# Strassen's weight sums ahead of the value, x's sums in a part's second couple: the order of two engines' queues in a float32 block on one Trainium2 core

## The reference

```
for l in range(2):
    x = x + 0.5 * swiglu(rms_norm(x, norm_ffn1[l]), ffn1_w_gate[l], ffn1_w_up[l], ffn1_w_down[l])
    x = x + hybrid_mixer(...)
    x = x + 0.5 * swiglu(rms_norm(x, norm_ffn2[l]), ffn2_w_gate[l], ffn2_w_up[l], ffn2_w_down[l])

swiglu(x) = (silu(x @ w_gate) * (x @ w_up)) @ w_down      # 1024 -> 2816 -> 1024, float32
```

## Time and profile before

| | us |
|---|---|
| three runs | 2627.64, 2631.72, 2637.26 (median 2631.72) |
| the profiled execution | 2631.17 |
| its span in the profile | 2629.4 |
| busy in it: PE, DVE, ACT, POOL | 2509.1 (95%), 1686.7 (64%), 1042.7 (40%), 248.3 (9%) |

### The profile page before, as it was taken

The page is one execution under the profiler, slowest core; times in us unless marked ns, Lnnn a source line. Parts: engine busy times, 40 slices in busy tenths (PEclk is TensorE's granted clock), DMA queues, the critical chain, the costliest instruction groups (busy, mean ns, idle before and its releaser), DMA issues. The chain is left out here.

```text
span 2629.4 us, 36570 instructions
## 1 busy us (share of the span) xinstructions
PE 2509.1 (95%) x14533; PEld 2120.8 (81%) x14533; DVE 1686.7 (64%) x2268; ACT 1042.7 (40%) x1434; POOL 248.3 (9%) x178
## 2 busy tenths in 40 slices
PE   7997997999999999999999999999999999999998
PEld 6876776888887878778888878888887777788886
DVE  5355996667675443658676787777743446777776
ACT  4344884333243234544343343333412255433333
POOL 0002112600003300120000010000050001100000
PEclk9998998999999999999999999999999999999999
DMA  4215994322324321232323233232333213232322
GB/s 140 65 56 208 399 412 159 96 89 97 97 91 134 101 73 52 77 97 72 98 98 105 85 97 97 96 98 96 120 108 88 66 35 98 85 101 92 110 83 80
DMA packets 88897, 292.72 MB, mean 111 GB/s; under 512 B 11523, under 2 KB 16531, under 8 KB 88467
## 3 DMA queue, kind: packets, MB, share of 16 engines
q1 hardware_dynamic: 81634, 264.10, 31.3%
q0 software_dynamic: 6224, 23.60, 2.3%
q10 hardware_dynamic: 864, 2.62, 0.2%
HBM read 276.12 MB, written 12.58 MB: 110 GB/s over the span
## 5 line engine op out<-in xcount | busy, mean ns | idle before, releaser
L507 DVE TENSOR_TENSOR w_lo<-w_raw,w_hi 128x1024 fp32r<-128x1024 f32 (+2 forms) x372 | 456.5, 1228 | 155.5 <-ACT w_hi L502 154.2
L551 PE MATMUL bank_l<-xg_hi,w_hi 128*128 128x512 f32 (+1 forms) x1312 | 515.5, 393 | 17.4 <-DVE w_lo L507 15.3
L502 ACT ACTIVATE w_hi<-w_raw 128x1024 fp32r<-128x1024 f32 (+2 forms) x372 | 370.7, 1005 | 364.5 <-PE bank_l L551 342.7
L551 PE MATMUL bank_l<-xg_lo,w_hi 128*128 128x512 f32 (+1 forms) x1312 | 510.0, 389 | 0.0
L551 PE MATMUL bank_l<-xg_hi,w_lo 128*128 128x512 f32 (+1 forms) x1312 | 507.1, 387 | 0.0
L551 PEld LDWEIGHTS bank_l<-xg_hi,w_hi 128*128 128x128 f32 x1312 | 247.5, 189 | 77.5 <-DVE w_lo L507 15.3
L551 PEld LDWEIGHTS bank_l<-xg_lo,w_hi 128*128 128x128 f32 x1312 | 247.3, 189 | 52.9 <-issue 2.2
L551 PEld LDWEIGHTS bank_l<-xg_hi,w_lo 128*128 128x128 f32 x1312 | 247.7, 189 | 52.1
L551 PE MATMUL bank_l<-hid_hi_ff,w_hi 128*128 128x512 f32 x704 | 279.2, 397 | 0.6 <-DVE hid_lo_ff L637 0.6
L551 PE MATMUL bank_l<-hid_hi_ff,w_lo 128*128 128x512 f32 x704 | 278.7, 396 | 0.0
L551 PE MATMUL bank_l<-hid_lo_ff,w_hi 128*128 128x512 f32 x704 | 276.6, 393 | 0.0
(11 more groups left out here) (436 smaller groups left out, 4810.0 us busy)
## 6 DMA issues: line engine op xcount, KB each, us to landing
w_raw<-in_ff_gate SPq DMA_DIRECT2D x88, 512.0 KB
expert_raw<-in_experts SPq DMA_DIRECT2D x81, 512.0 KB, 19.8
w_raw<-in_in SPq DMA_DIRECT2D x80, 512.0 KB
w_raw<-in_ff_down SPq DMA_DIRECT2D x64, 512.0 KB
up_raw<-in_ff_up SPq DMA_DIRECT2D x52, 512.0 KB, 4.6
w_raw<-in_ff_up SPq DMA_DIRECT2D x36, 512.0 KB
w_raw<-in_out SPq DMA_DIRECT2D x24, 512.0 KB
w_raw<-in_ff_down SPq DMA_DIRECT2D x32, 384.0 KB
```

The source lines that it names most:

```text
L502: act.activation(split_memory(i)[0], split_part(i), ACT.Copy).then_inc(*panel_hi.done(i))
L507: dve.tensor_tensor(lo, split_part(i), hi.bitcast(F32), ALU.subtract).then_inc(*panel_lo.done(i))
L551: done = pe.matmul(dst, w[:, c * cols:(c + 1) * cols], moving, start=c == 0 and n == 0, stop=c == kc - 1 and n == 2)
```

## The change

For the plain couple ahead of a couple by seven (j = 2, 5, 10, 13, 18), the order on DVE was S1, S3, value, S2, S4, rest of the value, rest of pair 0. It becomes S1, S3, S2, S4, rest of pair 0, value, rest of the value. On ACT the rounding of pair 0 comes before that of the value.

x's sums: T1 and T3 were made in the part's second couple (j = 1, in ff1_0 j = 6) behind the gate's scaling and the panel split, T2 and T4 in the third (j = 2, in ff1_0 7). Now T1 and T3 are made ahead of the second couple's gate scaling, T2 and T4 behind its panel split, and only their rests but for T1's stand in the third couple. On ACT, T1 and T3 are rounded ahead of `round_ahead(up)`, T2 and T4 behind it, all in the second couple.

```
--- before.py
+++ after.py
@@ -2008,21 +2008,21 @@
                         continue
                     gate, up = ff_keys(stage, j)
                     round_ahead(act, gate)
-                    if j == SEVEN[stage][0] - 1:
-                        round_x_sum(act, stage, "T2")
-                        round_x_sum(act, stage, "T4")
                     if j == 0 and before == "n":
                         first_root_act(act)
                     elif j == 0:
                         root_of_sum(act, before)
                     silu_act(act, stage, j)
-                    round_ahead(act, up)
                     if j == SEVEN[stage][0] - 2:
                         round_x_sum(act, stage, "T1")
                         round_x_sum(act, stage, "T3")
-                    hidden_act(act, stage, g, i, j)
+                    round_ahead(act, up)
+                    if j == SEVEN[stage][0] - 2:
+                        round_x_sum(act, stage, "T2")
+                        round_x_sum(act, stage, "T4")
                     if by_seven_next(stage, j):
                         round_sums(act, stage, j + 1, 0)
+                    hidden_act(act, stage, g, i, j)
                     j += 1
                 for m in range(DC):
                     round_ahead(act, ff_down(stage, g, m))
@@ -2150,10 +2150,12 @@
                         continue
                     gate, up = ff_keys(stage, j)
                     rest_ahead(dve, gate)
+                    if j == SEVEN[stage][0] - 2:
+                        make_x_sum(dve, stage, "T1")
+                        make_x_sum(dve, stage, "T3")
                     if j == SEVEN[stage][0] - 1:
-                        make_x_sum(dve, stage, "T2")
-                        make_x_sum(dve, stage, "T4")
-                        rest_of_x_sum(dve, stage, "T3")
+                        for name in ("T3", "T2", "T4"):
+                            rest_of_x_sum(dve, stage, name)
                     if j == 0 and before == "n":
                         first_root_dve(dve)
                     if j == 0:
@@ -2165,27 +2167,20 @@
                         *taken.done(gate))
                     rest_ahead(dve, up)
                     if j == SEVEN[stage][0] - 2:
-                        make_x_sum(dve, stage, "T1")
-                        make_x_sum(dve, stage, "T3")
+                        make_x_sum(dve, stage, "T2")
+                        make_x_sum(dve, stage, "T4")
                         rest_of_x_sum(dve, stage, "T1")
-                    if j == SEVEN[stage][0] - 1:
-                        rest_of_x_sum(dve, stage, "T2")
-                        rest_of_x_sum(dve, stage, "T4")
                     if by_seven_next(stage, j):
-                        for name in ("S1", "S3"):
+                        for name in ("S1", "S3", "S2", "S4"):
                             sum_of_weights(dve, stage, j + 1, name)
+                        rest_of_sums(dve, stage, j + 1, 0)
                     dve.wait_ge(*func.upto((stage, j)))
                     dve.wait_ge(*used.upto(panel_of[up]))
                     if j:
                         dve.wait_ge(*split_lo.upto((stage, j - 1)))
                     dve.tensor_tensor(val[:, :], ff_banks(up).of(up)[:, :], gate_value, ALU.mult).then_inc(
                         *taken.done(up))
-                    if by_seven_next(stage, j):
-                        for name in ("S2", "S4"):
-                            sum_of_weights(dve, stage, j + 1, name)
                     rest_of_value(dve, (stage, j), hid_lo[:, i, :], hid_hi[:, i, :], val[:, :])
-                    if by_seven_next(stage, j):
-                        rest_of_sums(dve, stage, j + 1, 0)
                     j += 1
                 for m in range(DC):
                     key = ff_down(stage, g, m)
```

## The result

| | before | after |
|---|---|---|
| median of the runs, us | 2629.68 (4 runs, 2626.43 to 2637.26) | 2609.67 (4 runs, 2607.42 to 2610.08) |
| profiled execution, its span | 2631.17, 2629.4 | 2607.42, 2605.6 |

The ratio is 0.9919, with a 95% interval of 0.9903 to 0.9934: 20 us faster, between 17 and 26. The forecast was 2615, in a range of 2607 to 2623.

A forecast was written before the change was run, and what follows sets the result against it. PE, busy 95% of the span, was taken to set the time. Fifteen waits removed, -17.4, and x's sums, +0.8, gave -16.6: 2631.17 to 2614.6, plus 0.4 for the median, 2615 us; range 2607 to 2623.

The forecast's parts named there:

- +4.3: Behind a plain couple, PE can start S2 T2 4.3 us after S1 starts, with 1.5 us to spare.
- 15 x 1.16 = 17.4: PE's fifteen waits of 1.16 us at S2 T2, for the rest of pair 0, all vanish: 17.4 us off the path.
- the clock rival: Behind couple 3's waits in some of three parts PE's clock stays up: -4 us, giving 2611; chance 0.14.
- -0.5: Couple 3 of ff2_0 and of ff2_1: PE starts 0.5 us earlier in each, S1 +0.27 less 0.8.
- A new wait of some 1.3 us: In ff1_1 PE waits 1.3 us for couple 1's value at couple 2's up product; its S2 T2 wait becomes 4.4.
- +0.7: In ff1_0 PE's 0.56 us wait for couple 7's rest grows by 0.7, or part shows at the down product's start.
- 3.6: DVE idles 3.6 us ahead of the panel rest in couple 1 of ff2_0.
- I leave the 6.4 as it is: The lower clock behind the three long waits costs 6.4 us beside them, and this stays unchanged.
- +0.8: Net of moving x's sums over all four parts: 0.8 us slower, bounds -2.4 to +8.
- the wait moves to pair 1: PE waits at S1 T1 instead, spare there only 0.8 us; half of 17.4 goes, 2623; chance 0.10.
- some 0.75: Smallest later spare, at pair 1 of the second couple by seven: 1.7 us before, some 0.75 after.
- Slower: ACT rounds T1 and T3 before the next panel, DVE stalls, the bank frees late: +20 against -17.4, 2634; chance 0.03.

The follow-up runs named there:

- The changed kernel again: The changed kernel with nothing edited, timed beside the kernel before: 2611.86 us, ratio 0.9923.
- value-ahead-of-pair-0 kernel: Against the changed kernel, DVE takes the value behind the four weight sums and ahead of pair 0's rest: 2611.31 us, ratio 0.9917 to the kernel before.
- the spread kernel: Against the changed kernel, ACT rounds the next panel ahead of x's sums; DVE makes T2, T4 before the panel's rest and moves their rests: 2593.01 us, ratio 0.9854.
- x's sums alone: Changed kernel with weight sums and value back in the old order, only x's sums moved: 2635.57 us, ratio 1.0021 to the kernel before.
- first half alone: Against the kernel before, only S2, S4 and pair 0's split go ahead of the value, x's sums unmoved: 2608.76 us, ratio 0.9912.

## Why the forecast came out as it did

**The fifteen places: the mechanism right, the term too small.** The prediction's step was that from S1 pair 0 is ready after +4.3; it is 4.30, and the wait is gone in all fifteen. The price was wrong: "15 x 1.16 = 17.4" should have been 15 x 1.42 = 21.3. PE's timeline before, around that wait (the middle row, 1239.66, stands in the earlier trace rows), and after:

```profile
1238.22 0.28 PE L1848 MATMUL bank_s<-xg_hi,w_lo 128*128 128x256 f32 x1
...
1239.88 0.28 PE L1848 MATMUL bank_s<-xs_lo,ws_hi 128*128 128x256 f32 x1
```

```profile
1232.47 0.28 PE L1848 MATMUL bank_s<-xg_hi,w_lo 128*128 128x256 f32 x1
...
1232.70 0.28 PE L1848 MATMUL bank_s<-xs_lo,ws_hi 128*128 128x256 f32 x1
```

Starts of these matmuls are 0.12 apart. Before, 1238.22 to 1239.88 is 1.66 for two steps; after, 1232.47 to 1232.70 is 0.23. The difference is 1.43, and 1.42 by the stretches. The idle time shown, 1.16, runs from the end of the last matmul, 0.28 behind its start, of which 0.16 overlaps with the next when there is no wait; and the first start behind a wait is followed by the next at 0.22, not 0.12. So a wait costs its idle time and 0.26. The waits of 1.01 confirm it: stretches of 21.11 against 19.84, 1.27 = 1.01 + 0.26. Between the forecast's sum, -16.6, and that of the parts, -22.2, lie 5.6 us, and this mis-sized term is 3.9 of them. The medians moved by 20.0, and 2609.7 is 5.3 below the forecast; they spread from one set of executions to the next (the kernel before: 2631.7 in the three that the forecast started from, 2629.7 in four), so the accounting goes by the parts. That the time lies in the range is in part luck: the low end was put there for the clock rival, and what used that room was this term above all.

**Couple 3.** "-0.5" in ff2_0 and ff2_1: the waits shrank by 0.51 and 0.49. "A new wait of some 1.3 us" in ff1_1: 1.53, and 4.34 behind it where I said 4.4. ff1_0 "+0.7": +0.7, and in the form given in brackets, at the product's start. DVE's idle time ahead of the panel rest: 3.54, foreseen as 3.6. These steps hold. Only the new wait in ff1_1 was priced too low: at 1.53 and 0.27 it cost 1.8, not 1.3.

**The clock.** "I leave the 6.4 as it is" was wrong by about 2 us. Stretches behind the three long waits, after (columns as in the earlier trace rows):

```profile
1199.90:1202.90 3.00, 2.99 (x14) 2.99 (x15) 2.05 (x3) 2.41 (x4) 0.00 (x0) 0.51 0.40 156
1561.50:1564.90 3.40, 3.40 (x17) 3.40 (x18) 2.45 (x3) 2.81 (x5) 0.00 (x0) 0.54 0.31 124
2275.50:2278.70 3.20, 3.15 (x15) 3.15 (x16) 2.25 (x3) 2.57 (x4) 0.00 (x0) 0.52 0.37 151
```

The lower level came behind each of them, as the page "TensorE: Matmul & The Clock Gate" of the Trainium skill (section "Why this matters for your kernels") says of waits amid a kernel, but in ff1_1 and ff2_1 it lasted some 3 us and not 6.1 and 5.1. What it cost can be taken from the starts of the matmuls, 0.21 apart at the lower level and 0.12 at full clock: 1.5, 2.9 and 2.4 us before, 1.6, 1.6 and 1.4 after, 2.2 less. With the 0.5 that the new wait in ff1_1 cost beyond its price, that is the -1.7 by which the parts' beginnings came out at -0.9 and not +0.8.

Is this luck? The changed kernel again has the short form at all three waits. Over the waits at L1848 in all profiles, the long form (20 to 28 slow starts, 2.0 to 2.9 us) came behind seven of the nine waits of 4.6 us and more, and behind one of the fifteen of 2.2 to 4.5 us, that of 4.29 in ff2_1 of the value-ahead-of-pair-0 kernel; all others had 13 to 17. So shorter waits went with the short form, in nearly all cases but not in all. No run isolates the cause, and it stays open. The rival that the clock stays up was wrong: even waits of 2.25 bring it down.

**The other rivals.** No wait at S1 T1 showed, so "the wait moves to pair 1" did not happen; the spare there is 0.7. For pair 1 of the second couple by seven the prediction had "some 0.75" left; it is 0.4 and in places 0.3. The forecast survived that, but it is the spare that the spread kernel used up. "Slower" had its mechanism right, as x's sums alone show, but at +3.4, not 20, and about half of that in ff1_1 alone. What I did not see beforehand is that this mechanism made the change smaller than its first half alone.

## What to carry to other kernels

When a wait in an in-order queue ends late, look for the instruction in the chain that stands behind something it doesn't need (here S2 behind the up product): its place is worth the whole wait, the places of its neighbours next to nothing. When work is moved to fill one engine's idle time, check what the partner engine does with it: T1 and T3 filled DVE's 1.56 us but put 1.90 of ACT's rounding ahead of a panel. Price a wait of PE by the distance of starts across it, not by the idle time that the profile prints.

## What the runs showed of the hardware

- A wait on PE between back-to-back matmuls of 256 columns costs 0.26 us beyond its printed idle time (1.16 and 1.42; 1.01 and 1.27).
- At L1848, PE's granted clock fell to the 1.2 GHz level behind every wait of 2.25 us and more, and stayed at 2.4 GHz behind the fifteen of 1.16. It need not fall at once: it did 0.8 and 1.2 us behind the waits of 2.25. How long it stays low differs at one and the same wait: 3.2 us behind the first of 4.63, 6.1 and 5.1 behind the others.
- The engines' queues repeat to some hundredths of a microsecond from one execution to the next: the stretch of 19.84 showed (19.79 to 19.85) in every kernel wherever PE didn't wait in it.
